# Two blocks without GpSimd's drain, and no wait for the gathered rows ahead of the stores in the expert loop

## The reference, cut to what matters

```python
h = _layernorm(concat([meta, x]), ln0_g, ln0_b)
mix = _mixer(h, w_in, sinks, conv_w, w_attn_out, w_conv_out, w_o)
h = _layernorm(alpha * h + mix, ln1_g, ln1_b)
# _hier_moe: softmax over 4 groups, the best group; in it the best 2 of 8 experts
xs = xt[tok_s]                                   # token rows, sorted by expert
a = silu(ragged_dot(xs, w_gate, sizes)) * ragged_dot(xs, w_up, sizes)
ys = ragged_dot(a, w_down, sizes) * weight
out = zeros_like(xt).at[tok_s].add(ys)
h = _layernorm(alpha * h + out, ln2_g, ln2_b)    # returned without the meta rows
```

## Time and profile before

| | us |
|---|---|
| median of three runs | 4183.0 (4179.87 to 4188.52) |
| the profiled execution | 4175.41 |
| its span, first to last instruction | 4173.4 |
| PE busy | 4066.0 (97%) |
| DVE / ACT / POOL busy | 2071.5 / 1444.6 / 742.2 |
| mixer, to the barrier of line 633 | 0 to 2619.4 |
| route, to the barrier of line 1360 | 2619.4 to 2647.9 |
| experts | 2647.9 to 4173.3 |

### The profile page before, as it was taken

The page is one execution under the profiler, slowest core; times in us unless marked ns, Lnnn a source line. Parts: engine busy times, 40 slices in busy tenths (PEclk is TensorE's granted clock), DMA queues, the critical chain, the costliest instruction groups (busy, mean ns, idle before and its releaser), DMA issues. The chain is left out here.

```text
span 4173.4 us, 60976 instructions
## 1 busy us (share of the span) xinstructions
PE 4066.0 (97%) x20066; PEld 3392.6 (81%) x20067; DVE 2071.5 (50%) x3202; ACT 1444.6 (35%) x2625; POOL 742.2 (18%) x1020
## 2 busy tenths in 40 slices
PE   8999999999999999999999999799999999999997
PEld 7888888888888888888888887587888888788885
DVE  4554443443443443433443344677656566656664
ACT  2422311311311311311311311466556566655553
POOL 2000010000001001001001001233333334333333
PEclk9999999999999999999999999899999999999998
DMA  8787456456456455555555555676656566665562
GB/s 256 243 305 246 144 202 203 158 195 196 166 199 187 170 201 182 175 197 186 178 192 191 174 193 200 232 250 231 242 190 211 191 213 235 233 203 193 198 215 81
DMA packets 278468, 840.53 MB, mean 201 GB/s; under 512 B 47952, under 2 KB 99408, under 8 KB 226688
## 3 DMA queue, kind: packets, MB, share of 16 engines
q1 hardware_dynamic: 228400, 716.61, 50.3%
q0 software_dynamic: 49936, 121.90, 8.7%
HBM read 717.60 MB, written 178.45 MB: 215 GB/s over the span
## 5 line engine op out<-in xcount | busy, mean ns | idle before, releaser
L1116 PE MATMUL bank<-hT_hi,w_slot 128*128 128x512 f32 x2176 | 862.2, 396 | 5.5 <-DVE w_slot L899 5.0
L1118 PE MATMUL bank<-hT_hi,w_slot 128*128 128x512 f32 x2176 | 848.8, 390 | 0.0
L1117 PE MATMUL bank<-hT_lo,w_slot 128*128 128x512 f32 x2176 | 848.1, 390 | 0.0
L1769 PE MATMUL e_bank<-e_w_hi,e_xT_hi 128*128 128x512 f32 x1312 | 519.7, 396 | 11.2 <-DVE e_xT_lo L1691 9.9
L1771 PE MATMUL e_bank<-e_w_hi,e_xT_lo 128*128 128x512 f32 x1312 | 512.4, 391 | 0.0
L1770 PE MATMUL e_bank<-e_w_lo,e_xT_hi 128*128 128x512 f32 x1312 | 511.3, 390 | 0.0
L1696 DVE TENSOR_TENSOR e_w_lo<-e_raw,e_w_hi 128x1024 fp32r<-128x1024 f32 x382 | 444.6, 1219 | 119.2 <-ACT e_w_hi L1646 113.8
L1116 PEld LDWEIGHTS bank<-hT_hi,w_slot 128*128 128x128 f32 x2176 | 409.0, 188 | 103.1 <-issue 21.8
L1118 PEld LDWEIGHTS bank<-hT_hi,w_slot 128*128 128x128 f32 x2176 | 408.9, 188 | 87.1
L1117 PEld LDWEIGHTS bank<-hT_lo,w_slot 128*128 128x128 f32 x2176 | 409.5, 188 | 81.3
L1646 ACT ACTIVATE e_w_hi<-e_raw 128x1024 fp32r<-128x1024 f32 x376 | 366.3, 1054 | 2.0 <-issue 2.0
(11 more groups left out here) (337 smaller groups left out, 6713.4 us busy)
## 6 DMA issues: line engine op xcount, KB each, us to landing
w_slot<-split_weights SPq DMA_DIRECT2D x353, 1024.0 KB, 4.8
e_raw<-in_w_exp_gate_dram SPq DMA_DIRECT2D x128, 512.0 KB, 5.7
e_raw<-in_w_exp_up_dram SPq DMA_DIRECT2D x128, 512.0 KB, 6.2
e_raw<-in_w_exp_down_dram SPq DMA_DIRECT2D x128, 512.0 KB, 5.3
split_weights<-w_slot SPq DMA_DIRECT2D x50, 1024.0 KB, 5.7
h_rows<-h_rows SPq DMA_DIRECT2D x64, 512.0 KB, 7.7
x_rows<-in_x_dram SPq DMA_DIRECT2D x32, 512.0 KB, 5.5
raw<-in_w_in_dram SPq DMA_DIRECT2D x30, 512.0 KB, 7.0
```

Source lines behind the costliest of these rows:

```text
L1116: pe.matmul(out, hi, x_hi, start=first, stop=False)
L1117: pe.matmul(out, hi, x_lo, start=False, stop=False)
L1118: return pe.matmul(out, lo, x_hi, start=False, stop=last)
L1769: pe.matmul(out_p, hi, x_hi, start=first, stop=False)
```

## The change

The blocks of `route` and of `experts` are opened with `no_gpsimd_drain=True`: the other engines still run their DRAIN, GpSimd doesn't, and the barrier is made by semaphores alone. In `gather_rows` the wait for the landing of the rows is taken out; one wait for all of them is put at the end of POOL's program. The rows' other waiter, PE's `transposes`, keeps its own wait.

```diff
-        with nc.Block() as block:                      # route
+        with nc.Block(no_gpsimd_drain=True) as block:
...
-        with nc.Block() as block:                      # experts
+        with nc.Block(no_gpsimd_drain=True) as block:
...
                     po.indirect_dma_start(out=rows[:, :], out_offset=None, in_=h1[0:TOK + S, :],
                                           in_offset=bass.IndirectOffsetOnAxis(ap=x_at[:, 0:1], axis=0))\
                       .then_inc(rows_in, 16)
-                    hold(po, rows_in, g * 16 + 16)
...
                 store_rows(total - 2)
                 deviation(total - 1)
                 store_rows(total - 1)
+                hold(po, rows_in, total * 16 + 32)
                 hold(po, rows_out, total * 16 + 48)
```

## The result

The changed kernel took 4142.5 us, median of four runs (4138.4 to 4146.6), beside 4183.3 for the kernel before on the same chip (4179.9 to 4188.5): ratio 0.9902, 95% interval 0.9888 to 0.9915, a gain of 40.8 us. The forecast was 4156, and its range ended at 4146; the gain was 27.2 by the sum and half as much again in the measurement. On three occasions the changed kernel ran 14 times in all and took one of two levels: three times 4138 to 4139, eleven times 4145 to 4148. Against the kernel before on the same chip the gain was 40.8 us, then 39.4 and 32.7; the last time the kernel before itself was faster, with a median of 4177.8.

The account below looks back on a forecast made before the run. PE was taken to bound the expert loop, with POOL at about its pace without reserve. Last drain 9.3, `route`'s drain 0.5 and the rows' wait 17.4 sum to 27.2 us: 4183.0 to 4156, range 4146 to 4172.

Parts of the forecast that it names:

- The last drain: POOL's DRAIN at the program's end, after the last store: nothing runs beside it, so removal gains its length, 9.3 us.
- Rival A: At the kernel's end, the last drain's time comes back outside the span; 4165 us, chance 0.12.
- The drain of `route`: At `route`'s end: without POOL's drain PE starts the first transposes earlier; 0.5 us taken, range 1.3 to -3.0.
- the collision that I put at 0.8 us: At `experts`' start: SP's loads go out beside the first gather; its landing may grow from 4.4 to 5.2 us.
- The wait for rows: POOL's expert loop: removal takes 4.9 us from each turn; PE's waits on rows, low parts and `prod` go, 17.4 us.
- 3.0 us of `down`: PE's wait in the expert loop on the count that lets `down` start; left out of the gain.
- the 12.8 us "that no wait is named for": Expert loop: PE time between 33.2 us above the floor and 20.4 of named waits; left out of the gain.
- The delays of POOL's issues: Stores moved under DVE's work: each could be held for one DVE instruction, 1.2 us; trace showed 0.8 more at most.
- The upper bound of 28: Expert loop: gain from moving the rows' wait if nearly all of the 33.2 us above the floor goes.
- B: Expert loop: POOL's relief doesn't reach PE, as DVE and ACT are themselves in a chain; gain 4, 4169 us, chance 0.17.
- C: POOL's loop: the next indirect transfer can't start while the first is under way; only drains gain, 4173 us, chance 0.06.
- D: Software queue: the partial sums' landing grows by more than 4.9 us; 28 us slower, 4211 us, chance 0.05.

## Why the prediction was right in kind and wrong in size

**The last drain**: 9.3 taken, 9.3 measured. Rival A, that the time comes back behind the span, is false: in all profiled executions the time is the span plus 1.7 to 2.1 us, with the drain or without. The rule cited from the Trainium skill, "Runtime: NRT & Kernel Launch", section "The ~15µs preamble/postamble breakdown", that a ring reset is paid behind each kernel in any case, has about the same size as what lies between time and span, 2.0 us before and 1.7 after; that it is this reset no run shows.

**The drain of `route`**: 0.5 taken, of a range of 1.3 to -3.0. The gather landed after 4.6 us beside SP's loads, so the collision that I put at 0.8 us took 0.3, and the start gained 1.2. The first tile gained 1.1 more, which I had no term for: PE runs it at half clock (1.2 GHz) up to 2658 before, and at full clock (2.4 GHz) from within 2653 to 2656 after. The windows of the changed kernel (PEclk is the last column but two) show it; in the kernel before, 2655 to 2658 still stands at 0.51.

```profile
2650.00:2653.00 3.00, 2.53 (x6) 2.05 (x7) 3.00 (x4) 1.28 (x1) 2.23 (x3) 0.50 1.05 409
2653.00:2656.00 3.00, 3.00 (x13) 2.40 (x13) 2.83 (x4) 0.00 (x0) 0.43 (x1) 0.89 1.03 389
```

But these 2.3 us are not safely the drain's. From line 633's barrier to the second transposes the three traces with drain and wait as before take 46.8 to 47.0 us; the two with the wait moved and the drain kept take 45.0 and 44.7; the nine without the drain 44.2 to 44.7. A part of this comes before either edit can act. In four traces, among them both with the moved wait and the drain, PE's product of line 1490 inside `route` was shorter by 1.1 to 1.3 us, and `route`'s gather left 22.7 us behind line 633's barrier in place of 23.9. The product in the kernel before, and in the kernel with the wait alone moved:

```profile
2635.05 5.57 PE L1490 MATMUL r_lists<-r_listed,r_hot_lo 128*128 128x196 f32 x16 [9.09 <-ACT r_listed L1405]
2635.87 4.50 PE L1490 MATMUL r_lists<-r_listed,r_hot_lo 128*128 128x196 f32 x16 [9.10 <-ACT r_listed L1405]
```

From 2635 to 2641 the granted clock was 0.51 in the first; over the same product in the second it was 0.72 (2635.8 to 2641.8). Why the clock was back earlier there is open. Among the ten traces with the late gather the missing drain gives 2.0 to 2.5 us, among the four with the early one 0.3 to 0.8. The drain's removal is worth that much at the start, 0.3 to 2.5 us against the 0.5 that I took, and it costs the stand before the last store, 2.6 to 2.8, which comes one transfer earlier without it. That is a cost that no row of before showed. Taken together the part is worth nothing that could be measured: 4144.4 with the drain put back, against 4142.5 to 4145.2 without.

**The wait for rows**: 17.4 taken, 26.3 measured in the two profiled executions. This is the step that failed, by its size. Its mechanism held in the links that I had named: POOL's wait for rows at nil, its waits for others at 8 us a tile (about 5 forecast), DVE's wait for `base` at 3.4 (under 20), PE's for rows at 0 and for low parts at 1.2 (under 2), the tiles at 1439.0 (1440 to 1450, so just below). What I left out of the sum went as well. I had set aside 3.0 us of `down` as another's; 0.9 is left. And I had set aside the 12.8 us "that no wait is named for"; of the 6.9 us now above the floor, 3.6 have a name, so 3.3 remain. They were not a loss of their own but came and went with the stops: 22 named stops with 12.8, and 3 with 3.3, are 0.6 and 1.1 us for each, and in all 14 traces it is 0.6 to 1.3. What they consist of is known in part. It isn't the clock that was won: it falls once in either loop, by the same amount, 0.34 x 5 = 1.7 us. The windows are of the changed kernel (after stops of 1.54 and 1.19 us at 2884.10 and 2885.95), then of the kernel before (after the stop of 2.45 us of the earlier trace rows; here length, busy PE, PEclk, DMA share, GB/s):

```profile
2885.00:2890.00 5.00, 4.05 (x11) 3.24 (x12) 4.74 (x5) 5.00 (x7) 0.66 (x1) 0.66 0.02 7
2910.00:2915.00 5.00, 5.00 (x16) 0.66 0.87 315
```

By the starts of the transposes about 6 of the 9.5 us lay in tiles with a named stop and 3.5 in tiles without one. A part of the 6 is the view's: it counts idle time from the modelled end of a matmul, 0.16 us after the next one could have begun, and the first matmul after a stop is followed after 0.33 us and not 0.23 (2895.28 and 2895.61 in the kernel before). That is some 0.26 us a stop, an estimate, so 5 us for 19 stops. The rest has no explanation here.

So the account is 16.8 of named waits (20.4 less 3.6) and 9.5 that went with them.

The delays of POOL's issues that the prediction feared for the moved stores didn't come in this execution: the issue of the store of `both` took at most 1.13 us and that of `finished` 1.08 (1.95 and 1.12 before). DVE's instructions of the 1.2 us that it gave for such a delay are the TENSOR_TENSOR of L1696 (1219 ns in the mean), and no trace shows these in a two-port mode. Its comparison of 1.2 us with a delay of 0.8 decides nothing.

**From one execution to the median.** The profiled execution of before was 7.9 us below the median of its four runs, that of after 3.4 below its own: 36.3 + 7.9 - 3.4 = 40.8. I carried the gain of an execution below the median over to the median unchanged. The loop of the kernel before wasn't typical in it: the two other traces with the wait in its old place and `base` in use have 43.8 and 41.7 us above the floor, not 33.2. The second of these, at 4175.3 us with the last drain gone, would be at 4184.6 with its 9.3 us, about the median of the kernel before. So what makes the kernel before take 4184 and not 4175 is most likely the late loop itself, though no second trace of that kernel was taken. A change that takes the lateness away takes this with it. Between such a loop and the changed kernel's usual one (13.1 and 13.2 above the floor) lie 29 to 31 us. The upper bound of 28 was made from 33.2, and the range used 26 of it; from 42 it would have been some 37, and the range would have held the result.

Rivals B (relief that doesn't reach PE) and C (nothing in the loop) are false by the waits. D, a slower queue, too: the stores of `both` land after 4.1 us in the median (4.5 before) and the gathers of rows after 5.1 (5.2 before, the medians over the loop).

## To carry to other kernels

An engine that waits for its own transfers and hardly ever for another engine can still set the pace. Add up its turn: where that equals the bounding engine's turn it has no reserve, and its lateness shows as small stops of others in several places. These are one loss and must not be costed one by one. A wait taken from such a turn is not won in full, either: 4.9 us less a turn brought 26.3 / 81 = 0.3 us a tile. With each named stop went 0.6 to 1.3 us without a name, and a gain that is a lateness removed is to be reckoned from the typical execution, not from the fastest. A wait is best put where nothing stands behind it that others need.

## What the runs showed that was not expected

- In the expert loop POOL stands some 2.6 us longer than usual (3.5 in place of 0.9) once in 110 of its indirect transfers, at a fixed transfer, whatever lies between; 110 transfers are 483 to 492 us in the changed kernel. Moved by one transfer it can be hidden. No run shows what POOL does there, nor why `route`'s drain shifts it by one.
- A drain of POOL at a block's end takes 4.1 us without any transfer before it, 6.1 at the mixer's last block after 56, 4.5 to 4.8 at `route`'s end after 58, and 9.3 after all 391. So its length doesn't follow the number of transfers alone, and what it waits for is not shown in the traces.
- With the drains gone and the wait kept, the median fell by 15.3 us where the landmarks give 8.8. The executions of that loop lie 15 us apart (4163.7 to 4179.5), those of the changed one 10; whether the start moves which tiles of a late loop are late stays open.
- POOL's issue of one and the same store took 1.1 us in five of the 14 traces and 4.5 in nine, the kernels with the wait in its old place included, and this parts the two levels of the changed kernel, 6 us apart.
